# The expert loop of a decoder layer: weight loads in runs of 16 KiB per partition, six transfers of 2 MiB per expert

## The reference

```python
def moe_ffn(x, w_router, b_router, w_gate_up, b_gate_up, w_down, b_down):
    logits = (xt @ w_router + b_router).astype(jnp.float32)
    top_val, top_idx = lax.top_k(logits, TOP_K)
    top_w = jax.nn.softmax(top_val, axis=-1)
    gates = jnp.sum(jax.nn.one_hot(top_idx, N_EXPERTS, dtype=jnp.float32) * top_w[..., None], axis=1)

    def expert_step(acc, params):
        wgu, bgu, wd, bd, g = params
        hgu = xt @ wgu + bgu
        gate = jnp.minimum(hgu[:, :D_EXPERT], SWIGLU_LIMIT)
        up = jnp.clip(hgu[:, D_EXPERT:], -SWIGLU_LIMIT, SWIGLU_LIMIT)
        y = ((up + 1.0) * (gate * jax.nn.sigmoid(SWIGLU_ALPHA * gate))) @ wd + bd
        return acc + g[:, None].astype(y.dtype) * y, None
...
h = h + merged @ w_out[l]
hn = rmsnorm(h, norm_ffn_g[l])
h = h + moe_ffn(hn, ...)
return rmsnorm(h, norm_final_g)
```

## Time and profile before

| | |
|---|---|
| median of 3 runs (lowest, highest) | 1243.33 us (1241.56, 1244.72) |
| the profiled execution, its own time | 1241.16 us |
| its span, first to last instruction | 1239.3 us |
| TensorE matmuls busy | 1121.8 us, 91% |
| read from memory | 435.74 MB |
| DMA packets | 86628, of 437.11 MB |
| granted TensorE clock, mean | 0.987 |

### The profile page before, as it was taken

One profiled execution on the slowest core, in us unless ns is written; L12 is line 12 of the kernel. 1 busy time (PEld: TensorE's weight loads), 2 busy tenths in 40 slices (PEclk: granted clock), 3 DMA queues, 4 the chain that ended last, 5 costly groups with the idle time before them and its releaser, 6 DMA issues.

```text
span 1239.3 us, 15513 instructions
## 1 busy us (share of the span) xinstructions
PE 1121.8 (91%) x6044; PEld 444.4 (36%) x6044; DVE 205.8 (17%) x420; ACT 167.0 (13%) x326; POOL 18.6 (1%) x68
## 2 busy tenths in 40 slices
PE   7999999958999999999999999999999998898885
PEld 6676444433333332323333233333333332322321
DVE  1301222141112111111111111111111111111111
ACT  2274222140000000000000000000000000000002
POOL 1010000000000000000000000000000000000000
PEclk9999999978999999999999999999999999999998
DMA  9922123338999999999999999999999999999994
GB/s 334 386 75 109 51 111 140 135 136 333 407 417 418 418 417 418 418 417 418 418 419 418 417 418 418 418 417 418 417 418 417 417 417 417 417 418 418 417 418 194
DMA packets 86628, 437.11 MB, mean 353 GB/s; under 512 B 7704, under 2 KB 7760, under 8 KB 53744
## 3 DMA queue, kind: packets, MB, share of 16 engines
q1 hardware_dynamic: 84880, 434.19, 86.3%
q10 hardware_dynamic: 1424, 1.57, 0.5%
q0 software_dynamic: 304, 1.06, 0.2%
HBM read 435.74 MB, written 1.06 MB: 352 GB/s over the span
## 4 chain that ended last, share of the span: by engine, by line
SPq 47%; PE 37%; DMA 9%; issue 4%; DVE 2%; ACT 1%; DVEq 0%
SPq L315 26%; SPq L310 20%; PE bank L1019 10%; DMA ring<-in_w_gate_up_dram 7%; PE bank L862 7%; PE bank L859 5%; PE bank L1049 3%; PE bank L945 2%; PE bank L956 2%; DMA ring<-in_w_down_dram 2%; PE bank L1002 2%; PE bank L993 1%; PE bank L917 1%; PE bank L839 1%; PE bank L1038 0%
## 5 line engine op out<-in xcount | busy, mean ns | idle before, releaser
L1019 PE MATMUL bank<-ring,gates 128*64 128x512 f32 x2048 | 476.9, 604 | 18.2 <-DMA ring<-in_w_gate_up_dram 15.3
L1049 PE MATMUL bank<-ring,gates 128*64 128x512 f32 x1024 | 244.2, 603 | 60.0 <-DMA ring<-in_w_down_dram 59.9
L1019 PEld LDWEIGHTS bank<-ring,gates 128*64 128x64 f32 x2048 | 135.1, 137 | 276.9 <-issue 191.3
L771 DVE TENSOR_SCALAR gates<-bank 128x512 f32<-128x512 f32 x32 | 22.1, 691 | 790.2 <-PE bank L1019 790.2
L1049 PEld LDWEIGHTS bank<-ring,gates 128*64 128x64 f32 x1024 | 64.0, 136 | 238.8 <-DMA ring<-in_w_down_dram 152.8
L862 PE MATMUL bank<-ring,colsT 128*128 128x512 f32 x192 | 85.0, 597 | 0.0
L1002 PE MATMUL bank<-gates,scatter_w 64*128 64x512 f32 x256 | 63.6, 615 | 0.8 <-ACT gates L570 0.7
L566 ACT ACTIVATE gates<-gates 128x512 f32<-128x512 f32 x32 | 20.2, 630 | 296.6 <-DVE gates L771 296.6
L859 PE MATMUL bank<-colsT,ring 128*128 128x256 f32 x256 | 58.8, 388 | 0.0
L993 PEld LDWEIGHTS bank<-onehot,qkT 128*128 128x128 bf16 x1536 | 47.7, 99 | 27.9 <-issue 25.2
L570 ACT ACTIVATE gates<-bank 128x512 f32<-128x512 f32 x32 | 19.1, 597 | 260.9 <-PE bank L1049 260.9
(11 more groups left out here) (167 smaller groups left out, 500.3 us busy)
## 6 DMA issues: line engine op xcount, KB each, us to landing
ring<-in_w_gate_up_dram SPq DMA_DIRECT2D x256, 1024.0 KB, 20.6
ring<-in_w_down_dram SPq DMA_DIRECT2D x128, 1024.0 KB, 24.6
ring<-in_w_in_dram SPq DMA_DIRECT2D x10, 2048.0 KB, 18.7
ring<-in_w_out_dram SPq DMA_DIRECT2D x1, 4096.0 KB, 14.1
ring<-in_w_proj_sb_dram SPq DMA_DIRECT2D x1, 2048.0 KB, 7.6
ring<-in_w_proj_moba_dram SPq DMA_DIRECT2D x1, 2048.0 KB, 13.4
resid<-in_x_dram SPq DMA_DIRECT2D x2, 512.0 KB, 3.7
bias<-u_scratch POOLq DMA_DIRECT2D x1, 1024.0 KB, 12.4
```

The lines of the kernel that those rows point to most:

```text
L771: V.tensor_scalar(gate_t, bank[4][:, :], SWIGLU_LIMIT, None, ALU.min).then_inc(gate_rd, 1)
L1019: ins = mm(bank[4 + i][SLOTS * c:SLOTS * (c + 1), :], xeT[:, k, :], ring[:, k, i * D + c * CH:i * D + (c + 1) * CH], start=False, stop=k = ...
L1049: ins = mm(bank[6][SLOTS * c:SLOTS * (c + 1), :], rows, ring[:, KD + s, j * D + c * CH:j * D + (c + 1) * CH], start=k == 0, stop=k == KD - 1)
```

## The change

The ring has 6 slots of 16 KiB per partition. The rows of w_gate_up are dealt out in another order: slot s (0 to 3) holds rows 256 s to 256 s + 255, and partition p gets the two neighbouring rows 256 s + 2 p and 256 s + 2 p + 1, one run of 16 KiB. A w_down slot (4, 5) holds 512 rows, partition p the four neighbouring rows 4 p to 4 p + 3 of them, again one run of 16 KiB. Each transfer is 2 MiB, and TensorE waits for one, and releases one, at every second k (w_gate_up) or every fourth (w_down).

So that the contraction meets the same rows, the activations are dealt out likewise: the pieces are stored with even and odd columns apart (`by_rows`, `piece_rows`: the copies and subtractions step by two elements on one side), the gains come from a new small load `gslot` in that order, and `hidden_columns` transposes every fourth column of `h_t` at a time.

```diff
-    RING = 12
-    SLOT = 2 * D
+    RING = 6
+    GU = 4
+    SLOT = 4 * D
...
+        gslot = sb("gslot", [P, KD // 2, 2])
...
+        piece_rows = [p.rearrange("p t (s r q) -> p (t s) q r", r=2, q=P) for p in pieces]
+
+        def by_rows(t):
+            return t.rearrange("p t (s q r) -> p (t s) q r", q=P, r=2)
...
-            gu = w_gate_up[0].rearrange("e (k p) n -> e k p n", p=P)
-            dn = w_down[0].rearrange("e (k c p) n -> e k p c n", p=P, c=2)
+            gu = w_gate_up[0].rearrange("e (s p r) n -> e s p (r n)", p=P, r=2)
+            dn = w_down[0].rearrange("e (s p r) n -> e s p (r n)", p=P, r=4)
 
             def load_slot(e, s):
 
...
+                src = gu if s < GU else dn
+                q = s if s < GU else s - GU
+                piece = src[e, q] if isinstance(e, int) else src[bass.ds(e, 1), q].rearrange("o p n -> p (o n)")
+                sp.dma_start(ring[:, s, :], piece).then_inc(slot_in[s], 16)
...
-            def load_gate_up(e, done, first=0):
-                for k in range(first, KD):
-                    sp.wait_ge(gu_used, (e + done) * KD + (k + 1 - KD))
-                    load_slot(e, k)
+            def load_gate_up(e, done):
+                for s in range(GU):
+                    sp.wait_ge(gu_used, (e + done) * GU + (s + 1 - GU))
+                    load_slot(e, s)
...
+            with nc.allow_non_contiguous_dma(reason="two gains in a run"):
+                act.dma_start(gslot[:, :, :], norm_ffn_g[0].rearrange("(s p r) -> p s r", p=P, r=2)
+                              ).then_inc(late_in, 16)
...
-            nc.scalar.activation(pieces[0], scaled[:, :, :], ACT.Copy).then_inc(piece_rd, 1)
+            nc.scalar.activation(piece_rows[0], by_rows(scaled[:, :, :]), ACT.Copy).then_inc(piece_rd, 1)
...
-            V.tensor_tensor(res2, scaled[:, :, :], pieces[0], ALU.subtract).then_inc(piece_d, 1)
+            V.tensor_tensor(by_rows(res2), by_rows(scaled[:, :, :]), piece_rows[0], ALU.subtract).then_inc(piece_d, 1)
...
                 for k in ks:
-                    pe.wait_ge(slot_in[k], g * 16 + 16)
+                    if k % 2 == 0:
+                        pe.wait_ge(slot_in[k // 2], g * 16 + 16)
                     for i in range(2):
                         for c in range(2):
+                            n0 = (k % 2) * 2 * D + i * D + c * CH
                             ins = mm(bank[4 + i][SLOTS * c:SLOTS * (c + 1), :], xeT[:, k, :],
...
-                    ins.then_inc(gu_used, 1)
+                                     ring[:, k // 2, n0:n0 + CH], start=False, stop=k == KD - 1)
+                    if k % 2 == 1:
+                        ins.then_inc(gu_used, 1)
...
-                    ins = tp(bank[7][:, c * P:(c + 1) * P], h_t[:, c * P:(c + 1) * P], ident[:, :])
+                    ins = tp(bank[7][:, c * P:(c + 1) * P], h_t[:, c::4], ident[:, :])
```

More of the change, by code:

```diff
@@ L175, in chunk_w @@
             u = PLACE[c]
-            return ring[:, 2 * u:2 * u + 2, :].rearrange("p a b -> p (a b)").rearrange("p (k n) -> p k n", k=KD)
+            return ring[:, u, :].rearrange("p (k n) -> p k n", k=KD)
         def flat(u0, u1):
-            return ring[:, 2 * u0:2 * u1, :].rearrange("p a b -> p (a b)")
+            return ring[:, u0:u1, :].rearrange("p a b -> p (a b)")
         wp_sb = flat(4, 5).rearrange("p (k n) -> p k n", k=4)
@@ L301, in _ @@
             sp.dma_start(wo_sb, w_out[0].rearrange("(k p) n -> p k n", p=P)).then_inc(wout_in, 16)
-            gu = w_gate_up[0].rearrange("e (k p) n -> e k p n", p=P)
-            dn = w_down[0].rearrange("e (k c p) n -> e k p c n", p=P, c=2)
+            gu = w_gate_up[0].rearrange("e (s p r) n -> e s p (r n)", p=P, r=2)
+            dn = w_down[0].rearrange("e (s p r) n -> e s p (r n)", p=P, r=4)
             def load_slot(e, s):
[L308 to L319, removed]
+                src = gu if s < GU else dn
+                q = s if s < GU else s - GU
+                piece = src[e, q] if isinstance(e, int) else src[bass.ds(e, 1), q].rearrange("o p n -> p (o n)")
+                sp.dma_start(ring[:, s, :], piece).then_inc(slot_in[s], 16)
+            for s in (2, 3):
+                if s == 2:
                     sp.wait_ge(unit_ps, LAST_UNIT[9] + 1)
@@ L322, in _ @@
             sp.wait_ge(out_ps, 8)
[L323 removed]
+            for s in (4, 5):
                 load_slot(0, s)
             sp.wait_ge(out_ps, 12)
[L326 removed]
+            for s in (0, 1):
                 load_slot(0, s)
[L329 to L332 removed]
+            def load_gate_up(e, done):
+                for s in range(GU):
+                    sp.wait_ge(gu_used, (e + done) * GU + (s + 1 - GU))
+                    load_slot(e, s)
             def load_down(e, done):
[L335 to L337 removed]
+                for q in range(RING - GU):
+                    sp.wait_ge(dn_used, (e + done) * (RING - GU) + (q + 1 - RING + GU))
+                    load_slot(e, GU + q)
             def experts(done):
@@ L756, in take @@
                 return V.tensor_tensor(xeT, bank7.rearrange("p (k s) -> p k s", k=KD),
-                                       gcol[:, KD:2 * KD].rearrange("p (k o) -> p k o", o=1)
+                                       gslot[:, :, :].rearrange("p s (r o) -> p (s r) o", o=1)
                                        .to_broadcast([P, KD, SLOTS]), ALU.mult)
@@ L1042, in down @@
                 pe.wait_ge(hT_rd, g + 1)
-                for s in range(RING - KD):
-                    pe.wait_ge(slot_in[KD + s], g * 16 + 16)
-                    for j in range(2):
-                        k = 2 * s + j
-                        rows = hT[:, k % 4, SLOTS * (k // 4):SLOTS * (k // 4) + SLOTS]
+                for s in range(RING - GU):
+                    pe.wait_ge(slot_in[GU + s], g * 16 + 16)
+                    for j in range(4):
+                        k = 4 * s + j
+                        rows = hT[:, j, SLOTS * s:SLOTS * s + SLOTS]
                         for c in range(2):
                             ins = mm(bank[6][SLOTS * c:SLOTS * (c + 1), :], rows,
-                                     ring[:, KD + s, j * D + c * CH:j * D + (c + 1) * CH], start=k == 0,
+                                     ring[:, GU + s, j * D + c * CH:j * D + (c + 1) * CH], start=k == 0,
                                      stop=k == KD - 1)
```

18 lines of the change are left out of this document (8 added, 10 removed).

## The result

| | before | after |
|---|---|---|
| median of 6 runs each (lowest, highest) | 1244.15 us (1241.56, 1244.91) | 1249.88 us (1247.31, 1251.94) |
| ratio, with its 95% interval | | 1.0047 (1.0031 to 1.0064) |
| the profiled execution, its span | 1239.3 us | 1248.5 us |
| granted TensorE clock, mean | 0.987 | 0.976 |

Forecast were 1224 us, a range of 1213 to 1239, and 0.79 for faster. The kernel became slower, by more than the 0.3% that can be told from no change.

What follows compares the result with a forecast made beforehand. The DMA engines' byte rate was taken to bound the expert loop. Longer runs (-24.0) and coarser slots at start (+2.9) and tail (+2.0) summed to -19.1 us, giving 1224 us, range 1213 to 1239.

Steps and rivals of the forecast that it cites:

- D: Strided copies and subtractions ahead of the first gather: taken as 0, at most 3.4 us more.
- A: 16 KiB runs in the expert loop: 429 GB/s, an expert in 29.35 us, 24.0 us less in all.
- R1: Rival for the loop's loads: 16 KiB runs give nothing over 8 KiB, only w_down gains; 1238 us, chance 0.14.
- R2: Rival for the loop's loads: 16 KiB runs read slower, 416 GB/s for instance; 1251 us, chance 0.08.
- R3: Rival for the loop's loads: a packet's fixed part is smaller, a third of the price; 1240 us, chance 0.05.
- R5: Rival: the full 14 ns per packet are saved and B or C don't come; 1211 to 1214 us, chance 0.07.
- B: Coarser slots at the loop's start: the second refill is released later, delaying unbroken loading; +2.9 us.
- C: The tail behind the last landing: the last slot is 2 MiB, so down(31) ends later; +2.0 us.
- R4: Rival: larger slots let the DMA queue run dry in every expert; 1243 to 1248 us, chance 0.05.
- E: Four transposes per expert reading every fourth column: hidden in the loop, 0 to +0.7 us in the tail, taken as 0.
- F: The gslot load of 512 8-byte runs on ScalarE's queue before the attention: hidden by waits, 0.
- G: Half as many issues, semaphore waits and completions: SyncE and TensorE are not the limit, 0.

Runs made afterwards that it cites:

- read_steps: The changed kernel with its three copies and two subtractions walking bfloat16 in order and float32 by two elements; 1230.5 us, ratio 0.9905.
- weight_steps: The changed kernel with copies and subtractions in order and the gather's stationary operand read with a step of two; 1231.04 us, ratio 0.9886.
- before_jumps: The kernel before with only ScalarE's three copies walked in jumps of 128 elements on both sides; 1265.73 us, ratio 1.0178.
- wide_slots: 2 MiB transfers and six slots as in the changed kernel, rows in old order (8 and 4 KiB runs), no stepped copies or gslot load; 1250.14 us.
- fine_ends: free_tail with slot 0 of experts 1 and 2 filled and released in halves; 1223.45 us, ratio 0.9845.
- free_tail: gains_late with the last expert's w_down loaded into ring slots 0 and 1, its second piece in two halves; 1224.29 us, ratio 0.9845.
- gains_late: read_steps with the gslot load issued behind the b_down load, later on ScalarE's queue; 1230.41 us, one execution.
- copy_forms: The kernel before with nine ScalarE and three VectorE copies added behind the expert loop; ScalarE took 1.89 us in order, 9.3 to 9.7 for far bfloat16 writes.
- busy_tensor: free_tail with 57 matmuls of unused results in TensorE's idle stretches ahead of the loop and between experts 0 and 1; 1214.09 us, ratio 0.9776.

## Why the prediction was wrong, point by point

**D, the strided copies, is the step that failed.** The text says that copies and subtractions "step by two elements". That is true of neither: the float32 side is walked in order, and the bfloat16 side is written in pairs 256 bytes apart. The row chosen to bound it, VectorE's reduction at L724, reads float32; none of the rows shown has scattered 2-byte writes, so its factor of 1.4 bounded something else. For the steps that were meant it even holds (2.70 against 1.89 us). The three copies cost 7.3 us each more, 22.0 together, of which the 0.7 us of slack ahead of the second subtraction hid a little: +21.3 us instead of 0, with an upper bound given as 3.4. `read_steps`, `weight_steps` and `before_jumps` show it. The sign that the forecast named for this, a gather later than 271 us, came.

A page bears on it that I did not weigh. The Trainium skill, "SBUF — State Buffer", section "Door 1: The DMA port swizzle (why `[64,N]` ≈ `[32,N]`)", has 16-byte lines in the buffer: accesses to the same line run at full bandwidth, each crossing to a new one pays, so a step is free up to 4 elements of float32 or 8 of bfloat16. For bfloat16 writes the trace agrees in part: 9.32 us by 16 elements, but 2.70 by 2, which should be free, against 1.89 in order. The page gives no price, and for ScalarE's reads the trace hardly shows one (2.60 for pairs 512 bytes apart).

**A was right**, in mechanism and size. The period is 29.37 us for 29.35 forecast, the rate 428 for 429, and the packets of a long window in the loop show the runs uncut:

```profile
DMA packets 17646, 257.09 MB, mean 428 GB/s; under 512 B 1955, under 2 KB 1955, under 8 KB 1955
q1 hardware_dynamic: 17646, 257.09, 100.7%
```

These are 15,691 packets of 16 KiB in 600 us on 16 engines, 616 ns each, where 611 to 617 were forecast. R1, R2 and R3 are out, and so is R5's saving of 34 us, with 23.7 measured; `wide_slots` shows the complement.

**B and C came to 2.8 us where 4.9 were forecast, and one term was missing.** The first release came 2.0 us later after expert 0's start, as the coarser slot would have it. That the second refill decides, +2.9, wasn't seen in after (0.8 us less dry time there; why is not shown), and `fine_ends` gives back at most 1. C's path behind the last landing has +1.6 of 2.0. Not seen at all was that the DMA engines run dry in the tail, +4.2. C took the landings at the loop's pace as given and did not ask when their slots come free. R4 had the mechanism but placed it in every expert, where the share is 1.01; at the end, the last w_down loads wait for down(30), each for 2 MiB, and nothing else is left to load. `free_tail` shows it: 4.0 to 4.4 us for the dry time and the coarse last slot together.

**The clock was left out.** While ScalarE copied, TensorE lay idle:

```profile
267.00:308.00 41.00, 15.90 (x81) 7.32 (x83) 10.91 (x29) 21.04 (x11) 0.23 (x1) 0.51 0.00 0
```

A granted clock of 0.51 is the lower level, 1.2 GHz, for nearly all of these 41 us, with TensorE busy for 15.9 of them. In before's profiled execution it rose to the upper one, 2.4 GHz, in the b_down matmuls (3.97 us), here only behind them (7.19): +3.3 us. But short copies do not settle it: the same 7.19 stand in `free_tail`, `gains_late`, `weight_steps` and `wide_slots`, and in the kernel before itself in `copy_forms`. So the 3.3 us count against before's 1241 us group, and its median holds most of them already. That TensorE's idle stretches are what lowers the clock here is shown by `busy_tensor`, with 3.69. The Trainium skill, "TensorE: Matmul & The Clock Gate", Part 1, says that an idle TensorE falls to half clock and that the moment of return varies from run to run; the two groups of before's times agree.

**E was right**: the transposes' weight loads grew from 141 to 212 ns in the median, 0.1 us per expert, hidden. **F** cost about a microsecond and not 0: ScalarE's 3.80 us of waiting hid the load's own issue, but not the 4.04 us of the issue behind it on the same queue. The first copy starts at 258.35 instead of 257.13; in the three profiles with the early load it starts between 257.59 and 258.54, in the seven without it (`busy_tensor` left out) between 256.35 and 257.37, and `gains_late` against `read_steps` gives 0.8 us. **G was right** at nothing.

In sum by the profiles: forecast -19.1; D +21.3, the first copy's later start (F) +1.2, clock +3.3, tail dry +4.2, A 0.3 short, less 1.7 by which B (1.2 in all) fell short and 0.4 for C, gives 9.1 where 9.2 was measured. Two small sums of the forecast are off without weight for this: its chances add up to 1.01, and D's 3.4, E's 0.7 and 20% on A would make the main range 1219 to 1233.

## What to carry to other kernels

Before costing a strided copy, write down for each side which address the next element has, and its type: reading far apart costs little here, writing 2-byte elements 32 bytes or more apart takes ScalarE five times as long as writing them in order. Put the step where it is free, on the read side or in a matmul's stationary operand. When slots get larger, look at the first and the last refills as well as the middle, and when a chain of other engines leads up to a TensorE stretch, expect that it can start at half clock, or fill the idle time.

## What was not expected of the hardware

- ScalarE needs 9.2 to 9.7 us for 2048 bfloat16 elements per partition written 32 bytes or more apart, 1.9 in order; VectorE 5.4 and 1.2 (measured while ScalarE was copying); ScalarE in float32 4.0.
- A load of 512 runs of 8 bytes makes the next issue on ScalarE's queue take 4.0 us instead of 0.5.
- In three profiles (`weight_steps`, `wide_slots`, `gains_late`) the clock fell once more in the tail: behind a wait of 2.5 to 3.4 us for the last load the last 16 matmuls took 5.15 to 5.35 us instead of 3.65. In `read_steps`, behind 2.59 us, it did not.
- 57 matmuls that compute nothing used make the kernel about 10 us faster (1224.29 to 1214.09), with the granted clock at 1.00 through the router where it was 0.62.
- The straight line of 9.5 to 9.9 ns per packet holds up to 16 KiB, and 2 MiB per transfer gives nothing over 1 MiB with the same runs (418 GB/s in both).
